# Weight halves of the third block split before the first block's eviction, and the convolution's next high part cast before the block's activation

## What is computed

```
# first block, feed-forward and its norm
h = x * (1.0 + sc2) + sh2
f = jnp.square(jax.nn.relu(h @ w_m1[l] + b_m1[l])) @ w_m2[l] + b_m2[l]
x = layer_norm(DEEPNORM_ALPHA * x + g2 * f, ln2_g[l], ln2_b[l])

# second block, layer 0
def conformer_conv(h, w_in, dw, dw_b, ln_g, ln_b, w_out):   # h = rms_norm(x, conv_norm)
    u = h @ w_in
    a, b, z = jnp.split(u, 3, axis=-1)
    v = a * jax.nn.sigmoid(b)
    v = lax.conv_general_dilated(v, dw[:, None, :], ..., feature_group_count=WIDTH) + dw_b   # 31 taps
    v = jax.nn.silu(layer_norm_2(v, ln_g, ln_b))
    return (v * jax.nn.silu(z)) @ w_out
```

## Time and profile before

| | |
|---|---|
| median of 3 runs | 2652.67 us (2652.21 to 2653.29) |
| profiled execution | 2649.32 us |
| its span, first to last instruction | 2647.4 us |
| mean granted clock of TensorE | 0.982 |
| TensorE busy | 2541.5 us, 96% |
| VectorE busy | 1995.5 us, 75% |
| ScalarE busy | 1377.4 us, 52% |
| GpSimd busy | 826.5 us, 31% |
| chain that ended last | PE 86%, DVE 6%, issue 3%, DMA 2% |

### The profile page before, as it was taken

One profiled execution on the slowest core, in us unless ns is written; L12 is line 12 of the kernel. 1 busy time (PEld: TensorE's weight loads), 2 busy tenths in 40 slices (PEclk: granted clock), 3 DMA queues, 4 the chain that ended last, 5 costly groups with the idle time before them and its releaser, 6 DMA issues.

```text
span 2647.4 us, 42736 instructions
## 1 busy us (share of the span) xinstructions
PE 2541.5 (96%) x16588; PEld 2313.1 (87%) x16588; DVE 1995.5 (75%) x2574; ACT 1377.4 (52%) x2161; POOL 826.5 (31%) x765
## 2 busy tenths in 40 slices
PE   6799999999998999999999989999899999999989
PEld 3688888889987888888888879999789999999978
DVE  7889777878879885555555678998767888888865
ACT  0444334444455554445543466776556666666643
POOL 0100001002245420001111338886103666666630
PEclk8899999999999999999999989999999999999989
DMA  9988766887865886555555534444454444444434
GB/s 347 370 289 271 251 219 206 274 273 260 288 222 197 278 273 206 191 175 192 191 185 187 188 109 160 160 144 157 136 177 160 153 154 158 152 160 154 154 114 146
DMA packets 147009, 534.60 MB, mean 202 GB/s; under 512 B 16855, under 2 KB 17016, under 8 KB 146424
## 3 DMA queue, kind: packets, MB, share of 16 engines
q1 hardware_dynamic: 143480, 519.82, 58.4%
q0 software_dynamic: 3328, 12.06, 1.4%
HBM read 525.52 MB, written 6.29 MB: 201 GB/s over the span
## 4 chain that ended last, share of the span: by engine, by line
PE 86%; DVE 6%; issue 3%; DMA 2%; ACT 1%; POOL 1%; SPq 0%; POOLq 0%; DVEq 0%; ACTq 0%
PE ps L595 34%; PE ps L599 26%; PE ps L597 9%; PE ps L598 9%; PE ps L982 2%; DVE misc L1066 2%; DMA AF<-in_w_ada 2%; PE ps L657 1%; DVE wl L1045 1%; PE ps L728 1%; PE ps L740 1%; DVE ps L1524 1%; ACT wh L1775 1%; PE ps L635 1%; DMA ring<-in_w_in 1%
## 5 line engine op out<-in xcount | busy, mean ns | idle before, releaser
L1045 DVE TENSOR_TENSOR wl<-ring,wh 128x1024 fp32r<-128x1024 f32 x784 | 1034.1, 1331 | 374.0 <-ACT wh L1775 341.3
L599 PE MATMUL ps<-A,wl 128*128 128x256 f32 x4480 | 1265.0, 282 | 0.0
L1775 ACT CAST wh<-ring 128x1024 fp32r<-128x1024 f32 x784 | 816.9, 1047 | 365.5 <-PE ps L599 348.1
L599 PEld LDWEIGHTS ps<-A,wl 128*128 128x128 f32 x4480 | 857.7, 191 | 0.4
L595 PE MATMUL ps<-A,wh 128*128 128x512 f32 x2176 | 779.8, 402 | 22.9 <-DVE wl L1045 10.1
L597 PE MATMUL ps<-A,wh 128*128 128x256 f32 x2304 | 674.0, 293 | 15.3 <-DVE A L1049 9.8
L595 PE MATMUL ps<-B,wh 128*128 128x512 f32 x1792 | 640.1, 402 | 18.6 <-DVE wl L1045 9.0
L598 PE MATMUL ps<-A,wh 128*128 128x256 f32 x2304 | 653.4, 284 | 0.0
L595 PEld LDWEIGHTS ps<-A,wh 128*128 128x128 f32 x2176 | 413.0, 190 | 124.5 <-DVE wl L1045 11.1
L599 PE MATMUL ps<-B,wl 128*128 128x256 f32 x1792 | 503.2, 281 | 0.0
L597 PEld LDWEIGHTS ps<-A,wh 128*128 128x128 f32 x2304 | 443.0, 192 | 18.8 <-issue 10.0
(11 more groups left out here) (248 smaller groups left out, 2157.7 us busy)
## 6 DMA issues: line engine op xcount, KB each, us to landing
ring<-in_w_m SPq DMA_DIRECT2D x256, 512.0 KB, 4.5
ring<-in_hgrn_w_in SPq DMA_DIRECT2D x160, 512.0 KB, 3.8
ring<-in_w_ada SPq DMA_DIRECT2D x146, 512.0 KB, 5.2
ring<-in_w_in SPq DMA_DIRECT2D x144, 512.0 KB, 5.7
ring<-in_conv_w_in SPq DMA_DIRECT2D x96, 512.0 KB, 4.2
AF<-in_w_ada SPq DMA_DIRECT2D x46, 512.0 KB, 8.1
ring<-in_w_ab SPq DMA_DIRECT2D x32, 512.0 KB, 5.6
ring<-in_w_o SPq DMA_DIRECT2D x32, 512.0 KB, 5.5
```

Of the source, the lines that this page charges most:

```text
L599: return e.matmul(dst[:, 0:256], lo, x[:, 0, :], start=False, stop=last)
L1045: e.tensor_tensor(low[:], ring[SLOT[h]][:], hi[:].bitcast(F32), ALU.subtract).then_inc(s.lo, 1)
L1775: e.copy(wh[h % NSPLIT][:], ring[SLOT[h]][:]).then_inc(s.hi, 1)
```

## The change

Three things move; no arithmetic changes.

1. **Split order.** A new function `split_behind(n)` says which splits are issued behind block n where a stage begins by turns: behind block 0 now halves 3, 4 and 5, behind block 1 only 6, from block 2 on 2n+3 and 2n+4 as before. So half 5, the second of the third block, is split ahead of block 0's eviction. It holds for both passes of M1 and for CO. For CV, halves 4 and 5 are split right behind `normalise` and `operand`, ahead of the root and the reciprocal. For CO, half 3 is cast right behind CV's last tick, ahead of the last block's silu and the remaining norm steps, and subtracted after the first of those steps (before: both after all of them).
2. **In CV**, ScalarE's sigmoid or silu of block i-1 (`gate_block`) is issued behind the next half's cast and ahead of the next tick, instead of ahead of both.
3. **Steps.** TensorE's row sums of the first eight squared tiles go one step later, to steps 15 and 16 of tile 7, so `TAP_STEPS` is 17.

```diff
-TAP_STEPS = 16
+TAP_STEPS = 17
...
+def split_behind(n):
+    return (3, 4, 5) if n == 0 else (6,) if n == 1 else (2 * n + 3, 2 * n + 4)
...
-            if n == 7 and step in (14, 15):
-                g = step - 14
+            if n == 7 and step in (15, 16):
+                g = step - 15
...
@@ VectorE, M1
-                for part in range(2):
-                    if fh or 2 * n + part:
-                        lo(H_M1[fh] + 2 * n + part + 3)
-                    if part == 0 and fh == 0 and n == 18:
+                for j in split_behind(n):
+                    if fh or j > 3:
+                        lo(H_M1[fh] + j)
+                    if j == 2 * n + 3 and fh == 0 and n == 18:
                         bias(10)
...
         normalise(1, operand(gn, 2))
+        lo(H_CV + 4)
+        lo(H_CV + 5)
...
@@ VectorE, CV
-                if 2 * i + part:
+                if 2 * i + part > 2:
                     lo(H_CV + 2 * i + part + 3)
...
         for step in range(2 * len(N_CV) - NORM_FROM, NORM_STEPS):
+            if step == 2 * len(N_CV) - NORM_FROM + 1:
+                lo(H_CO + 3)
             norm_step(step)
...
@@ VectorE, CO
-            for part in range(2):
-                lo(H_CO + 2 * n + part + 3)
-                if part == 0 and n:
+            for j in split_behind(n):
+                if j > 3:
+                    lo(H_CO + j)
+                if n and j in (6, 2 * n + 3):
                     next_low(n - 1)
...
@@ ScalarE (M1 and CO as on VectorE, with hi)
         operand(gn, 2, square_scaled)
+        hi(H_CV + 4)
+        hi(H_CV + 5)
         w.wait_ge(s.ss, 2 + 16)
...
-        for i, n in enumerate(N_CV):
-            bank()
-            for part in range(2):
-                if 2 * i + part:
-                    hi(H_CV + 2 * i + part + 3)
-                conv_behind(2 * i + part)
+        def gate_block(n):
             if 16 <= n < 32:
...
+        for i, n in enumerate(N_CV):
+            bank()
+            for part in range(2):
+                if 2 * i + part > 2:
+                    hi(H_CV + 2 * i + part + 3)
+                if part == 0 and i:
+                    gate_block(N_CV[i - 1])
+                conv_behind(2 * i + part)
+        hi(H_CO + 3)
+        gate_block(N_CV[-1])
```

More of the change, by code:

```diff
@@ L2013, in scalar_program @@
                 pb = bank()[:, 256:512]
-                for part in range(2):
-                    if fh or 2 * n + part:
-                        hi(H_M1[fh] + 2 * n + part + 3)
+                for j in split_behind(n):
+                    if fh or j > 3:
+                        hi(H_M1[fh] + j)
                 w.wait_ge(s.mm, H_M1[fh] + in_step(n))
@@ L2155, in scalar_program @@
             bank()
-            for part in range(2):
-                hi(H_CO + 2 * n + part + 3)
-                if part == 0 and n:
+            for j in split_behind(n):
+                if j > 3:
+                    hi(H_CO + j)
+                if n and j in (6, 2 * n + 3):
                     next_operand(n - 1)
```

## The result

The changed kernel takes 2619.11 us (median of 4 runs, 2617.61 to 2622.22), the kernel before beside it 2652.44 us: a ratio of 0.9882, 95% interval 0.9868 to 0.9897. The forecast was 2628, its range 2624 to 2639. Two copies of the changed kernel gave the same again in later runs (2619.29 and 2618.36 us); over all nine of its runs the median is 2618.4. The kernel before ran 66 times, these four and 62 beside the experiments, with a median of 2650.2 us and single times from 2644.2 to 2655.6.

The account below looks back on a forecast made before the run. TensorE, busy 2541.5 of 2647.4 us, was taken as the bound, so only its idle and half-clock time could be won. Savings of 2.2 + 4.0 + 7.8 + 11.1 = 25.1 us from 2652.7 gave 2627.6, stated as 2628, range 2624 to 2639.

Parts of the forecast that it names:

- term for M1: M1, both passes: splitting half 5 earlier removes two waits for low parts, 1.2 + 1.0 = 2.2 us.
- 4.0 us at 1707: CV's wait for a padded tile at 1707.72: GpSimd's chain limits what is kept there to 4.0 us, bounds 2.0 and 6.4.
- the wait for L1601's tile: Sign in CV: the padded-tile wait at 1707.72 grows from 1.1 to about 2.4 us.
- the three signs: Failure if CV waits for padded tiles more than once, GpSimd's additions average over 1.2 us, or the clock falls inside CO.
- 5.3 us: Start of CV: splitting halves 4 and 5 earlier starts TensorE 3.6 us sooner and saves 1.7 us of slow clock.
- 7.8 us: Inside CV: waits for squares and a low part go, with slow clock: 2.6 + 1.1 + 4.1 us, bounds 4 and 8.
- 11.1 us: CO: first turn starts without a wait and second turn ends 11.5 us earlier, rounded to 11.1; bounds 6 and 12.
- So I count no slow clock: CO: no remaining wait is long, so no half-clock time was counted; one slow stretch would give back 1.7 us.
- Low rows bounding CO: Rival, 14%: inserted cast and subtraction push the chain of rows, so CO gives only 5 to 7 us; 2633 us.
- GpSimd no earlier: Rival, 12%: GpSimd's chain in CV does not start earlier in effect, so the 4.0 us go; 2632 us.
- The early cast still waiting: Rival, 7%: inside CV the early cast still waits, waits at 1831 and 1837 stay, CO gives only 7.7 us; 2636 us.
- GpSimd's additions stretched: Rival, 3%: denser VectorE work slows GpSimd's additions in CV from mean 1.07 to 1.50 us; slower, 2668 us.

Follow-up runs that it names:

- again_after: The changed kernel, unchanged, run again for a second trace and further times: 2619.29 us, ratio 0.9877 to the kernel before.

## Why the prediction was right and wrong

- **The step that failed.** The mechanism was right, waits went where they should, but the sum took waits and half-clock time as all that could change. Its term for M1, 2.2 us with bounds 1 and 2.2, is the one that measures far outside its bounds: 5.9 us, 0.9 in the first pass and 5.0 in the second, because TensorE's matmuls ran at another pace there. The next miss in size is "4.0 us at 1707", which measured 5.8. The rest is the starting point, which lay 2.5 us high, and 1.7 us in stages that nothing changed.
- **Which waits go: right.** Of the nine waits of the earlier trace rows all are gone. Of the signs to look for, two failed: the wait for L1601's tile did not grow, and VectorE's waits for casts fell from 34.1 to 18.0 us, not below 15. It is still 25 waits instead of 26, of 0.7 us on average instead of 1.3, so the loop got shorter and did not go. And of the three signs by which the prediction wanted to be called failed, two came: a padded tile is waited for twice in CV (0.62 and 0.31 us, less together than the 1.07 before), and the clock falls inside CO.
- **M1, "2.2 us": waits right, size wrong.** Both waits went, and half 6 is not late. But the first pass gave 0.9 us on average instead of 1.2 and the second 5.0 instead of 1.0. The step took every matmul outside the waits as equal in both kernels. They are not: the second pass of the kernel before lost 5.1 us to the slow pace in two of its three own traces and none in any of the changed kernel's. The earlier trace rows cannot show it; the count of matmuls in equal windows would have.
- **Start of CV, "5.3 us": right (5.4 at 1570).** 0.9 of it go back at once, at the first padded tile, a wait that the prediction did not have. "**4.0 us at 1707**": mis-sized. It is 5.8, and the wait, which was to grow from 1.1 to about 2.4 us, vanished. Alone the part keeps 3.2 us and its wait does grow to 1.48. The step expected GpSimd's first addition 2.1 us earlier, most of 2.7 us of waits for products gone, and 1 us lost to overlap. GpSimd ends tile 7 5.9 us earlier: 2.2 by its first addition, 2.1 by products, 1.3 by VectorE's sums, for which it no longer waits, 0.3 in small pieces, and the 1 us is not lost. The sums were left out of the step: "hardly at all" looks at products alone, and for sums GpSimd waited 10.8 us up to 1840, 1.3 of them ahead of tile 9. Alone the two parts give 3.2 and 1.3, together 5.8.
- **Inside CV, "7.8 us": right in sum (8.3), one cause wrong.** The square of tile 7 gave 2.3 us against 2.6, the rest of CV 6.0 against 5.2. But the prediction had the moved row sums cover the 2.59 us wait alone; without the move the wait is gone all the same. It was the order of casts in CV that made that square late, as it had the one at 1837; neither the start of CV nor CO alone removed either wait.
- **CO, "11.1 us": right in size (10.3).** The first turn starts without a wait, as said. Waits of 1.1, 0.4 and 1.8 us were expected in it; there are 1.77 and 0.62. The second turn has no wait of 0.3 us (0.8 expected). "So I count no slow clock" failed: 6.8 us at 0.50. In it TensorE's matmuls take twice as long, but low rows that would have been waited for come meanwhile, so it costs less than its length says: in again_after, the same kernel, the clock is down for 3.4 us instead of 6.8, and CO is only 0.2 us shorter. The sum is near because misses on both sides nearly cancel, which is in part luck.

```profile
1856.80:1860.20 3.40, 3.29 (x12) 2.39 (x11) 3.40 (x6) 2.17 (x5) 1.74 (x2) 0.50 0.39 117
1860.20:1863.60 3.40, 2.64 (x12) 1.81 (x12) 3.40 (x9) 3.12 (x8) 0.00 (x0) 0.99 0.11 45
```

- **"Behind CO nothing takes it back": right.** The recurrence takes 613.0 us in all six traces.
- **The starting point.** The median of the three runs shown, 2652.67, lies 2.5 us above the median of 66 (2650.2). From there the forecast's 25.1 us lead to 2625.1; measured are 2618.4. The 6.7 us are, to 0.2, 4.0 in the second pass of M1 (its pace), 2.3 in CV, 0.8 the other way in CO and 0.3 the other way in the first pass, and 1.7 in the two stages that nothing changed, which is within what traces of one kernel differ by there.
- **The rivals.** Low rows bounding CO: no, CO gave 10.3 us. GpSimd no earlier: no, it was earlier by more than I took. The early cast still waiting: no, 1831 and 1837 are gone. GpSimd's additions stretched: their mean is 1.04 us in the trace against 1.07, so a VectorE with fewer pauses did not slow them. The contention with the subtraction is real all the same, and it is more than the "few" of the prediction: 73 of the 192 additions of the kernel before take 1.36 to 1.79 us, and 71 of these 73 began while a subtraction of weights (L1045) ran and ended 0.6 us behind its end, nearly a whole addition later. The others take 0.74 us in the median. A subtraction that begins while GpSimd works takes 1.52 us instead of 1.22. The rule on shared interfaces (the Trainium skill, GPSIMD Engine Reference, 1. Specifications: GpSimd contends with VectorE instructions that have two SBUF inputs) agrees with this trace. But the number of such additions did not rise: 67 of 192 in the changed kernel. The clock, too, did as weighed: with the long waits gone it is 1.00 behind CV's start, and fell once more behind the one wait of 1.77 us that is left. The first row is from the grouped lines of GpSimd in the changed kernel, the two behind it are one subtraction and the addition beside it in the kernel before:

```profile
L2439 POOL TENSOR_TENSOR misc<-misc 128x256 f32<-128x256 f32 x192 | 198.8, 1035 | 37.0 <-ACT misc L2087 13.1 <-POOL misc L2439 0.4
...
1603.13 1.21 DVE L1045 TENSOR_TENSOR wl<-ring,wh 128x1024 fp32r<-128x1024 f32 x1
1603.27 1.67 POOL L2419 TENSOR_TENSOR misc<-misc 128x256 f32<-128x256 f32 x1
```

- **The range** ended at 2624 because its low end added the better bounds of waits and clock only. A stretch whose matmuls could run faster was not among them, and neither was the spread of the starting point. With 5.9 in place of 2.2 for M1 the low end would have been 2620.4.

## What to carry to other kernels

Before summing waits, divide: count the matmuls of equal full-clock windows in every stage, and where two equal stretches differ, keep the difference in the range, since a change anywhere in the stream can win or lose it. When two engines feed a third, a part that ends one engine's pauses and a part that starts the chain earlier support each other; try each alone in thought and then ask what the one does to the other's limit. And take a cast that a later subtraction waits for ahead of an activation that waits for that same engine: here this order alone was worth 13 of 24 us.

## What the hardware showed that was not expected

- Equal matmuls at full granted clock have two paces, 346.7 and 353.3 ns for 768 columns (1.9% apart), each kept until the stream is broken; the slow one is a cycle of three k-tiles (350, 361, 349 ns), the fast one of two (350, 343) or even. This kernel with its 2.5 ms of matmuls loses 5.1 us by it in one stage, in some of its executions.
- One inserted matmul of one column every 32 k-tiles changes the pace with a period of four (slow, slow, slow, fast); two, four or eight never did in fourteen breaks each. A single break of eight did end a slow stretch in the kernel before. What sets the pace was not found.
- The wait whose removal gave 1.2 us in M1's first pass had, in most traces, also ended a slow stretch: without it 1.7 us were lost in 12 of 13 traces.
- A GpSimd addition that begins during VectorE's subtraction of two operands in SBUF ends only 0.6 us behind the end of that subtraction (71 of 73 long additions before, 66 of 67 after).
